# A transformer block's MLP computed with seven half products in place of eight

## The chip, the cores and the metric

The kernel runs on one core of a Trainium2 chip, as one launch. The metric is the device time of that launch in microseconds (us). TensorE (PE) multiplies and accumulates in PSUM, VectorE (DVE), ScalarE (ACT) and GpSimd (POOL) work element by element, SyncE (SP) issues most of the DMAs. PSUM tiles ps_A, ps_B, ps_C and ps_D are 128x1024 float32 each, that is two halves of 128x512.

## The reference, cut to what matters

Two transformer blocks run on x (1 x 1024 tokens x 1024 features, float32). The change lies in the last layer: its MLP and the final norm, with D_FF = 4096.

```python
mix = jnp.concatenate([na_out.astype(x.dtype), ret_out], axis=-1)
x = x + mix @ w_out[l]
h = rms_norm_2(x, norm_mlp[l])
x = x + jnp.square(jax.nn.relu(h @ w_up[l])) @ w_down[l]
return rms_norm_2(x, norm_final)
```

## The kernel before

Activations lie transposed: X is [128, 8, 1024], eight tiles of 128 features by 1024 tokens. A float32 product is made of three products in a faster format: each operand is split into a rounded part (hi) and the rest (lo), and hi*hi + hi*lo + lo*hi is accumulated. `linear` makes one output tile of 128 features by 1024 tokens: 8 k-steps, 3 hi/lo products, 2 halves of 512 tokens, so 48 matmuls, alternating between the two halves of ps_A or ps_B. They are all recorded at line 525. A weight tile (128x1024, 512 KB) is loaded by SP into w_raw (L382), rounded to w_hi on POOL (L442) and its rest w_lo made by POOL (L435). Two such sets alternate; PE frees one by `lin_done`, POOL gives it by `w_ready`, PSUM tiles go by `ab_free`.

The MLP runs in four chunks (FF_CHUNKS) of 1024 inner features. `up` makes 8 tiles of h @ w_up from HA (hi and lo of the normed X). DVE takes each out with relu and the norm's factor rstd into ta (L2195), ACT squares it (L1534) and rounds it into HB_hi (L1536), DVE makes HB_lo (L2198). `down` makes 8 tiles from HB, and DVE adds each to X (L2204). That is 64 tiles, 3072 matmuls. Chunks but one run in hardware loops. The normed input is made while the layer's mixer output product (8 tiles) runs: DVE adds a tile to X (L1724), ACT scales and rounds it and squares it (L1025, L1029), DVE makes the lo part (L1589) and adds up the squares (L1593). The sum over features is a matmul with a tile of ones (L545), after the first `up` tile. ACT makes rstd from it by Ln and Exp (L1013, L1015).

After the last tile comes the final norm: squares (ACT L1547), their sum (DVE L2219), ones matmuls (L545), rstd, then the scaling of eight tiles, five on DVE (L2226) and three on POOL (L496), and eight output DMAs (L420).

Each engine runs its own program in order; only the semaphores tie them. The order in which an engine's code is written is the order of its work.

## Time and profile before

| | |
|---|---|
| median of 3 runs | 2687.0 us (2684.63 to 2688.97) |
| the profiled execution, its own time | 2685.58 us |
| its span, first to last instruction | 2683.8 us |
| MLP on PE, first to last matmul | 1955.35 to 2653.44 us of the span |
| PE busy over the span | 94% |

The span is what the trace shows; the time holds 1.8 us more that lie around it. Stages are given in microseconds from the span's start. "Idle before, releaser" in a row is the time that the engine stood still before the instruction and who ended it.

### The profile page before, as it was taken

Reading aid. Unit: us, or ns where it says so; the run is one execution under the profiler, and the core shown is the slowest. Engines: PE = TensorE matmul, PEld = TensorE weight load, DVE = VectorE, ACT = ScalarE, POOL = GpSimd, SP = SyncE. Lnnn points to the kernel's source line nnn. Section 1 sums busy time; section 2 is a strip of 40 time slices with the busy share of each in tenths; the row PEclk is TensorE's granted clock in tenths of the full one; section 3 lists DMA queues with packets and bytes.
Section 4 is the critical chain, followed back from the end, with each engine's and each line's share of the span. In section 5 each row is a group of like instructions: output and inputs, shape, how many; then the busy total and the mean of one; then the engine's idle time right before and its main releaser. Section 6 shows DMA issues by size and latency. Waiting matters only on the chain.

```text
span 2683.8 us, 31485 instructions
## 1 busy us (share of the span) xinstructions
PE 2525.6 (94%) x11924; PEld 1953.8 (73%) x11924; DVE 1249.2 (47%) x1673; ACT 849.0 (32%) x1263; POOL 852.5 (32%) x437
## 2 busy tenths in 40 slices
PE   7999669999999999998899999999999999999995
PEld 5877448776776677765767777787788888888884
DVE  6999863435545455454744655454421121121223
ACT  5555441324444444445332233213221010010111
POOL 2888743222222222221222221221333333333332
PEclk9999879999999999999999999999999999999998
DMA  3111201111111111111111211220111111111111
GB/s 124 48 47 43 77 21 47 67 38 53 39 37 36 31 36 39 44 36 29 34 57 46 50 44 33 81 71 24 47 47 48 48 55 48 47 47 47 47 50 67
DMA packets 70876, 129.48 MB, mean 48 GB/s; under 512 B 37880, under 2 KB 40952, under 8 KB 70776
## 3 DMA queue, kind: packets, MB, share of 16 engines
q1 hardware_dynamic: 30096, 107.27, 12.3%
q10 hardware_dynamic: 40680, 20.76, 3.4%
q8 instruction: 76, 1.25, 0.2%
q14 instruction: 24, 0.20, 0.0%
HBM read 117.39 MB, written 4.33 MB: 45 GB/s over the span
## 4 chain that ended last, share of the span: by engine, by line
PE 74%; DVE 10%; issue 6%; ACT 5%; POOL 2%; ACTq 1%; DVEq 0%; DMA 0%; SPq 0%; POOLq 0%
PE ps_A L525 34%; PE ps_B L525 27%; PE ps_B L599 2%; POOL ta L460 2%; PE ps_C L622 1%; PE ps_D L622 1%; PE ps_C L545 1%; PE ps_D L545 1%; PE ps_B L732 1%; ACT sc L1221 1%; DVE ssum L1593 1%; DVE ps_C L1639 1%; PE ps_B L545 1%; DVE sc L1774 1%; PE ps_C L708 1%
## 5 line engine op out<-in xcount | busy, mean ns | idle before, releaser
L442 POOL CAST w_hi<-w_raw 128x1024 fp32r<-128x1024 f32 x162 | 171.3, 1058 | 1657.8 <-PE ps_A L525 794.5
L435 POOL TENSOR_TENSOR w_lo<-w_raw,w_hi 128x1024 fp32r<-128x1024 f32 x188 | 467.2, 2485 | 60.2 <-ACT w_hi L1036 47.2
L525 PE MATMUL ps_A<-HA_hi,w_hi 128*128 128x512 f32 x960 | 314.7, 409 | 46.7 <-POOL HA_lo L484 21.1
L525 PE MATMUL ps_A<-HA_lo,w_hi 128*128 128x512 f32 x960 | 300.6, 395 | 0.0
L525 PE MATMUL ps_A<-HA_hi,w_lo 128*128 128x512 f32 x960 | 299.9, 394 | 0.0
L525 PE MATMUL ps_B<-HA_hi,w_hi 128*128 128x512 f32 x832 | 265.5, 400 | 3.6 <-DVE G L1620 3.3
L525 PE MATMUL ps_B<-HA_lo,w_hi 128*128 128x512 f32 x832 | 256.9, 390 | 0.0
L525 PE MATMUL ps_B<-HA_hi,w_lo 128*128 128x512 f32 x832 | 256.6, 390 | 0.0
L525 PEld LDWEIGHTS ps_A<-HA_hi,w_hi 128*128 128x128 f32 x960 | 176.5, 191 | 96.1 <-issue 47.5
L525 PEld LDWEIGHTS ps_A<-HA_lo,w_hi 128*128 128x128 f32 x960 | 182.9, 191 | 39.4
L525 PEld LDWEIGHTS ps_A<-HA_hi,w_lo 128*128 128x128 f32 x960 | 182.8, 190 | 39.6
L525 PE MATMUL ps_A<-HB_hi,w_hi 128*128 128x512 f32 x640 | 203.4, 399 | 7.0 <-DVE HB_lo L2063 4.2
L1534 ACT ACTIVATE sq<-ta 128x1024 f32<-128x1024 f32 x32 | 34.0, 1062 | 529.7 <-DVE ta L2195 529.7
L525 PE MATMUL ps_A<-HB_lo,w_hi 128*128 128x512 f32 x640 | 198.1, 391 | 0.0
L525 PE MATMUL ps_A<-HB_hi,w_lo 128*128 128x512 f32 x640 | 197.7, 390 | 0.0
L525 PEld LDWEIGHTS ps_B<-HA_lo,w_hi 128*128 128x128 f32 x832 | 156.3, 188 | 33.3
L525 PEld LDWEIGHTS ps_B<-HA_hi,w_lo 128*128 128x128 f32 x832 | 156.2, 188 | 33.2
L525 PEld LDWEIGHTS ps_B<-HA_hi,w_hi 128*128 128x128 f32 x832 | 152.0, 188 | 37.7 <-issue 8.6
L525 PE MATMUL ps_B<-HB_hi,w_hi 128*128 128x512 f32 x512 | 160.8, 395 | 0.0
L525 PE MATMUL ps_B<-HB_lo,w_hi 128*128 128x512 f32 x512 | 157.8, 389 | 0.0
L525 PE MATMUL ps_B<-HB_hi,w_lo 128*128 128x512 f32 x512 | 157.7, 389 | 0.0
L525 PEld LDWEIGHTS ps_A<-HB_hi,w_hi 128*128 128x128 f32 x640 | 118.4, 188 | 35.3 <-issue 8.2
(335 smaller groups left out, 3800.6 us busy)
## 6 DMA issues: line engine op xcount, KB each, us to landing
w_raw<-w_dram SPq DMA_DIRECT2D x188, 512.0 KB, 3.5
X<-x_dram SPq DMA_DIRECT2D x8, 512.0 KB, 8.0
X<-x_dram ACTq DMA_DIRECT2D x8, 512.0 KB, 7.2
out_dram<-X SPq DMA_DIRECT2D x8, 512.0 KB, 2.8
wp_sb<-wp_dram ACTq DMA_DIRECT2D x16, 128.0 KB, 2.0
qT<-q_in ACTq DMA_DIRECT2D x48, 32.0 KB
kT<-k_in ACTq DMA_DIRECT2D x48, 32.0 KB
p_A<-p_dram ACTq DMA_DIRECT2D x2, 512.0 KB, 3.9
```

Source lines behind the costliest of these rows:

```text
L435: pool.tensor_tensor(w_lo[q][:, :, :], w_raw[q][:, :, :], w_hi[q][:, :, :].bitcast(F32), ALU.subtract).then_inc(S[f"w_ready{q}"], 1)
L442: pool.tensor_copy(w_hi[q][:, :, :], w_raw[q][:, :, :]).then_inc(S["w_rounded"], 1)
L460: pool.tensor_tensor(accp[u][:, :], (tap_out[0] if j == 0 else accp[u])[:, :], tap_out[(j + 1) % 2][:, :], ALU.add).then_inc(S["pool_tap"], 1)
L525: op = pe.matmul(AB[b][:, cols], wt[:, w0 + k, :], act[:, k, cols], start=(first and k == ks[0] and step == 0), stop=(last and k == ks[-1] ...
L545: op = pe.matmul(ps[b][:, cols], m[:, :], src[:, cols], start=first, stop=last)
L599: op = pe.matmul(AB[b][:, cols], wp_sb[t][:, k, :], p_sb[k][:, cols], start=(k == 0), stop=(k == PLE_K - 1))
L622: op = pe.transpose(CD[b][:, c * P:(c + 1) * P], src(c), ident[:, :])
L708: op = pe.matmul(CD[slots[u]][d, T - P:T], V[:, k0 + c, d], pt[u % 2][:, (h * nk + c) * P:(h * nk + c + 1) * P], start=(c == 0), stop=(c = ...
L732: op = pe.matmul(AB[other][:, at:at + nk * P], qT[rows, u * P:(u + 1) * P], kT[rows, k0 * P:(k0 + nk) * P], start=True, stop=True)
L1221: op = act.activation(s, s, ACT.Exp, scale=-1.0, bias=st_at(g, u, h, 0), accum_out=st_at(g, u, h, 1))
L1534: act.activation(sq[:, :], ta[:, :], ACT.Square).then_inc(S["u_sq"], 1)
L1593: dve.tensor_tensor(ssum[:, :], ssum[:, :], sq[:, :], ALU.add).then_inc(S["ssum_added"], 1)
```

## The change

The MLP's two products are each cut into 2x2 blocks: output features, inner index and tokens each in two halves. In place of the eight block products of each such group come seven (Strassen's algorithm in Winograd's form), on sums and differences of blocks. One block product (`half_product`) is 12 matmuls of 128x128 by 128x512: 4 k-steps of 3 hi/lo products, all into one half of a PSUM tile. Products x = 1 to 7 are run in an order in which later ones accumulate onto earlier ones in PSUM ("running sums").

Up: 16 pairs of output tiles (UP_PAIRS), seven products each. Left blocks are weights (DVE makes s1 to s4 from the raw weights), ACT rounds each (up_w hi, a ring of five) and POOL makes its lo part. Right blocks are sums of halves of the normed X, formed once (HT, seven operands with hi and lo) at the end of the mixer's output product. ACT copies running sums out (`keep_p1`, `keep_u2`, `keep_p5`), DVE adds and applies relu (c11, c22, c12, b21), ACT squares, and DVE forms differences (t1, b12, t2, t4). The seven combinations per pair are stored to u_dram by SP, 256 KB each.

Down: the combinations are read back (`t_piece`, 512 KB each), split into hi and lo again on ACT and DVE, four operands in flight. Items are (products, chunk, pair of output tiles): 48 items of two products in three phases (1,2), (6,5), (7,3) and 16 items of product 4 alone. Weights of each pair are loaded again in every phase: 512 KB, 768 KB, 1 MB and 256 KB an item, a ring of three. DVE forms their sums (`form_item`: none, two, three and none), ACT rounds, POOL makes lo.

X is stored to memory ahead of the up products and loaded again in the down stage, since the up stage uses its place. The final norm is made for each half of the tokens; the second half's is made before the last items are done. Some other semaphores are merged, and the constant tile perm is no longer loaded. The loops of this part are gone from every program (PE's has 5016 rows in place of 3121).

```diff
+UP_PAIRS = FF_CHUNKS * KH
+UP_ORDER = [(0, x) for x in (1, 5, 6, 2, 7)]
+for _i in range(1, UP_PAIRS):
+    UP_ORDER += [(_i, 1), (_i - 1, 3), (_i - 1, 4)]
+    UP_ORDER += [(_i, x) for x in ((5, 6, 2, 7) if _i < UP_PAIRS - 1 else (6, 5, 7, 2, 3, 4))]
+UP_AT = {_s: _n for _n, _s in enumerate(UP_ORDER)}
+RING = 5
...
+PHASES = ((1, 2), (6, 5), (7, 3))
+CHUNKS = len(PHASES) * FF_CHUNKS
+ITEMS = CHUNKS * PAIRS
...
+            def up_weights(i):
+                c, b = divmod(i, KH)
+                for t in range(2):
+                    sp.dma_start(a_raw[i % 2][t][:, :, :], w[MLP_AT + 2 * KT * c + b + KH * t]) \
+                        .then_inc(S[f"a_loaded{i % 2}"], 16)
+            def store_u(i, x, tile):
+                c, b = divmod(i, KH)
+                sp.dma_start(u_dram[x - 1, c, :, b, :], tile[i % 2][:, :]).then_inc(S[f"u_stored{i % 2}"], 16)
+            def store_two(i):
+                sp.wait_ge(S["b_ready"], 4 * i + 2)
+                store_u(i, 1, b11)
+                store_u(i, 3, b22)
+            def store_five(i):
+                sp.wait_ge(S["t_formed"], 4 * i + 4)
+                store_u(i, 2, b21)
+                store_u(i, 5, t1)
+                store_u(i, 7, b12)
+                store_u(i, 6, t2)
+                store_u(i, 4, t4)
...
+            def t_piece(k):
+                t, h = divmod(k, 2)
+                if k < 2:
+                    sp.wait_ge(S["up_split"], UP_AT[(UP_PAIRS - 2, 4)] + 1)
+                elif k < 4:
+                    sp.wait_ge(S["up_split"], len(UP_ORDER))
+                else:
+                    sp.wait_ge(S["t_ready"], k - 3)
+                c = t // 2 % FF_CHUNKS if t < 2 * CHUNKS else t - 2 * CHUNKS
+                for q in range(2):
+                    sp.wait_ge(S[f"u_stored{q}"], 16 * 7 * (KH // 2) * (c + 1))
+                sp.dma_start(t_raw[k % 4][:, :, :], u_dram[T_ORDER[t] - 1, c, :, 2 * h:2 * h + 2, :]) \
+                    .then_inc(S[f"t_loaded{t % 2}"], 16)
...
+                kind, c, p = item(i)
+                if i < 2:
+                    sp.wait_ge(S["up_done"], UP_AT[(UP_PAIRS - 1, 7)] + 1)
+                elif i == 2:
+                    sp.wait_ge(S["up_done"], UP_AT[(UP_PAIRS - 1, 3)] + 1)
+                else:
+                    sp.wait_ge(S["down_split"], split_count(i - 2))
...
+            for i in range(UP_PAIRS - 1):
+                if i > 0:
+                    sp.wait_ge(S["up_split"], UP_AT[(i - 1, 4)] + 1)
+                    up_weights(i + 1)
+                store_two(i)
+                if i > 0:
+                    store_five(i - 1)
+            store_five(UP_PAIRS - 2)
+            for k in range(4):
+                t_piece(k)
+            for i in range(3):
+                down_weights(i)
+            store_two(UP_PAIRS - 1)
+            store_five(UP_PAIRS - 1)
+            for i in range(LAST):
+                if i >= 3:
+                    down_weights(i)
+                for k in t_pieces_after(i):
+                    t_piece(k)
+                if i == PAIRS + 1:
+                    for q in range(2):
+                        sp.wait_ge(S[f"u_stored{q}"], 16 * 7 * UP_PAIRS // 2)
+                    for k in range(KT):
+                        sp.dma_start(X[:, k, :], out[k]).then_inc(S[f"x_loaded{k}"], 16)
...
+            for s in range(len(UP_ORDER)):
+                hi, lo = up_w[s % RING]
+                pool.wait_ge(S["up_hi"], s + 1)
+                pool.tensor_tensor(lo[:, :, :], up_source(s), hi[:, :, :].bitcast(F32),
+                                   ALU.subtract).then_inc(S["up_split"], 1)
+            for i in range(LAST):
+                for j, x in enumerate(item(i)[0]):
+                    hi, lo = down_w[i % 3][j]
+                    pool.wait_ge(S["down_hi"], split_count(i) + j + 1)
+                    pool.tensor_tensor(lo[:, :, :], d_raw[i % 3][:, down_parts(x), :], hi[:, :, :].bitcast(F32),
+                                       ALU.subtract).then_inc(S["down_split"], 1)
...
-            def down():
-                def u_ready(k):
-                    pe.wait_ge(S["u_ready"], n.next("u_ready"))
-                linear(0, HB, pre=u_ready)
-                for t in range(1, KT):
-                    linear(t % 2, HB)
-            opening(0, HA)
-            for t in range(1, KT):
-                linear(t % 2, HA)
-            down()
-            with n.loop(pe, FF_CHUNKS - 1, w_ready0=8, w_ready1=8, ab_free0=8, ab_free1=8, u_ready=KT):
-                for t in range(KT):
-                    linear(t % 2, HA)
-                down()
-            norm_stats()
...
+            def half_product(bank, wt, ht, first, ready=None):
+                for k in range(KH):
+                    if ready:
+                        ready(k)
+                    for step, (a, b) in enumerate(((wt[0], ht[0]), (wt[0], ht[1]), (wt[1], ht[0]))):
+                        op = pe.matmul(bank, a[:, k, :], b[:, k, :], start=(first and k == 0 and step == 0),
+                                       stop=(k == KH - 1 and step == 2), skip_group_check=True)
+                return op
...
+            for s, (i, x) in enumerate(UP_ORDER):
+                q = i % 2
+                if x == 1:
+                    bank = AB[q][:, HALVES[0]]
+                    if i < 2:
+                        pe.wait_ge(S[f"ab_free{q}"], n.now(f"ab_free{q}"))
+                    else:
+                        pe.wait_ge(S["up_out"], OUT_AT[("r21", i - 2)] + 1)
+                if x == 6:
+                    bank = AB[q][:, HALVES[0]]
+                    pe.wait_ge(S["kept"], KEPT_AT[(1, i)] + 1)
+                if x == 7:
+                    bank = AB[q][:, HALVES[0]]
+                    pe.wait_ge(S["kept"], KEPT_AT[(6, i)] + 1)
+                if x == 4:
+                    bank = AB[q][:, HALVES[0]]
+                    pe.wait_ge(S["up_out"], OUT_AT[("c22", i)] + 1)
+                if x == 5:
+                    bank = AB[q][:, HALVES[1]]
+                    if i >= 2:
+                        pe.wait_ge(S["up_out"], OUT_AT[("c12", i - 2)] + 1)
+                if x == 3:
+                    bank = AB[q][:, HALVES[1]]
+                    pe.wait_ge(S["kept"], KEPT_AT[(5, i)] + 1)
+                if x == 2:
+                    bank = CD[0][:, HALVES[q]]
+                    if i == 0:
+                        pe.wait_ge(S["cd_free0"], n.now("cd_free0"))
+                    elif i >= 2:
+                        pe.wait_ge(S["up_out"], OUT_AT[("c11", i - 2)] + 1)
+                pe.wait_ge(S["up_split"], s + 1)
+                ready = (lambda k: pe.wait_ge(S["mlp_lo"], LO_AT[(x, k // 2 if x in (7, 4) else k)] + 1)) if i == 0 else None
+                half_product(bank, up_w[s % RING], HT[x], x in (1, 2, 5), ready).then_inc(S["up_done"], 1)
+                if (i, x) == (0, 6):
+                    norm_stats()
...
+            def round_up(s):
+                i, x = UP_ORDER[s]
+                if s >= RING:
+                    act.wait_ge(S["up_done"], s - RING + 1)
+                if x in (1, 2, 4):
+                    act.wait_ge(S[f"a_loaded{i % 2}"], 32 * (i // 2 + 1))
+                else:
+                    act.wait_ge(S["up_sum"], SUM_AT[(i, x)] + 1)
+                act.copy(up_w[s % RING][0][:, :, :], up_source(s)).then_inc(S["up_hi"], 1)
...
+            for i in range(1, UP_PAIRS):
+                s = UP_AT[(i, 1)]
+                round_up(s + 3)
+                squared(b22, i - 1, "r22")
+                round_up(s + 4)
+                keep_p1(i)
+                round_up(s + 5)
+                squared(b12, i - 1, "r12")
+                round_up(s + 6)
+                squared(b21, i - 1, "r21")
+                if i < UP_PAIRS - 1:
+                    keep_p5(i)
+                    round_up(s + 7)
+                    keep_u2(i)
+                    round_up(s + 8)
+                    round_up(s + 9)
+                else:
+                    keep_u2(i)
+                    keep_p5(i)
+                    round_up(s + 7)
+                    round_up(s + 8)
+                squared(b11, i, "r11")
...
+            def form_s1(i):
+                dve.wait_ge(S[f"a_loaded{i % 2}"], 32 * (i // 2 + 1))
+                if i > 0:
+                    dve.wait_ge(S["up_split"], UP_AT[(i - 1, 5)] + 1)
+                second = a_raw[i % 2][1]
+                dve.tensor_tensor(s1[:, :, :], second[:, 0::2, :], second[:, 1::2, :], ALU.add).then_inc(S["up_sum"], 1)
+                dve.wait_ge(S["up_sum"], SUM_AT[(i, 5)] + 1)
+            def form_s2_s3(i):
+                first, second = a_raw[i % 2]
+                if i > 0:
+                    dve.wait_ge(S["up_split"], UP_AT[(i - 1, 6)] + 1)
+                dve.tensor_tensor(s2[:, :, :], s1[:, :, :], first[:, 0::2, :], ALU.subtract).then_inc(S["up_sum"], 1)
+                dve.tensor_tensor(second[:, 0::2, :], second[:, 0::2, :], first[:, 0::2, :],
+                                  ALU.subtract).then_inc(S["up_sum"], 1)
...
+            def c11(i):
+                stage_free(i)
+                dve.wait_ge(S["up_done"], UP_AT[(i, 2)] + 1)
+                dve.wait_ge(S["kept"], KEPT_AT[(1, i)] + 1)
+                dve.tensor_tensor(b11[i % 2][:, :], p1[:, :], CD[0][:, HALVES[i % 2]], ALU.add).then_inc(S["up_out"], 1)
+                out(("c11", i))
+                relu(b11, i, 0, b11[i % 2][:, :])
...
+            def form_t(i):
+                q = i % 2
+                dve.wait_ge(S["b_ready"], 4 * i + 4)
+                dve.tensor_tensor(t1[q][:, :], b12[q][:, :], b11[q][:, :], ALU.subtract).then_inc(S["t_formed"], 1)
+                dve.wait_ge(S["t_formed"], 4 * i + 1)
+                dve.tensor_tensor(t2[q][:, :], b22[q][:, :], t1[q][:, :], ALU.subtract).then_inc(S["t_formed"], 1)
+                dve.tensor_tensor(b12[q][:, :], b12[q][:, :], b22[q][:, :], ALU.subtract).then_inc(S["t_formed"], 1)
+                dve.wait_ge(S["t_formed"], 4 * i + 2)
+                dve.tensor_tensor(t4[q][:, :], b21[q][:, :], t2[q][:, :], ALU.subtract).then_inc(S["t_formed"], 1)
...
+            c11(0)
+            r22(0)
+            for i in range(1, UP_PAIRS):
+                if i > 1:
+                    c22(i - 1)
+                    r22(i - 1)
+                form_s4(i)
+                c12_c21(i - 1)
+                if i < UP_PAIRS - 1:
+                    form_s1(i + 1)
+                    form_s2_s3(i + 1)
+                form_t(i - 1)
+                c11(i)
...
+            def form_item(i):
+                kind, raw = item(i)[0], d_raw[i % 3]
+                if kind in PHASES[1:]:
+                    dve.wait_ge(S[f"d_loaded{i % 3}"], down_loads(i))
+                if kind == (6, 5):
+                    dve.tensor_tensor(raw[:, A21, :], raw[:, A21, :], raw[:, A22, :], ALU.add).then_inc(S["down_formed"], 1)
+                    dve.wait_ge(S["down_formed"], sums_formed(i) + 1)
+                    dve.tensor_tensor(raw[:, A11, :], raw[:, A21, :], raw[:, A11, :],
+                                      ALU.subtract).then_inc(S["down_formed"], 1)
+                if kind == (7, 3):
+                    dve.tensor_tensor(raw[:, A21, :], raw[:, A21, :], raw[:, A11, :],
+                                      ALU.subtract).then_inc(S["down_formed"], 1)
+                    dve.tensor_tensor(raw[:, A12, :], raw[:, A12, :], raw[:, A22, :],
+                                      ALU.subtract).then_inc(S["down_formed"], 1)
+                    dve.wait_ge(S["down_formed"], sums_formed(i) + 2)
+                    dve.tensor_tensor(raw[:, A12, :], raw[:, A12, :], raw[:, A21, :],
+                                      ALU.subtract).then_inc(S["down_formed"], 1)
```

PE at the seam between two output tiles, before (HB is the inner operand; an "x2" row is the two halves of ps_A or ps_B):

```order
L525 MATMUL ps_B<-HB_hi,w_hi_57 128x512 x2
L525 MATMUL ps_B<-HB_lo,w_hi_57 128x512 x2
L525 MATMUL ps_B<-HB_hi,w_lo_59 128x512 x2
L532 REGISTER_ALU
L507 REGISTER_ALU
L525 MATMUL ps_A<-HB_hi,w_hi_56 128x512 x2
L525 MATMUL ps_A<-HB_lo,w_hi_56 128x512 x2
```

and in the change, at the seam between products 6 and 2 of the first pair (ht is the right operand, up_w the weights):

```order
L1199 MATMUL ps_A<-ht_hi,up_w_hi 128x512
L1199 MATMUL ps_A<-ht_lo,up_w_hi 128x512
L1199 MATMUL ps_A<-ht_hi,up_w_lo 128x512
L785 MATMUL ps_D<-ssum,ones 128x512 x2
L1199 MATMUL ps_C<-ht_hi,up_w_hi 128x512
L1199 MATMUL ps_C<-ht_lo,up_w_hi 128x512
```

A matmul no longer comes twice with the same weights: twelve different ones go to one half of a tile.

SP's queue in the MLP, before (a loop over two weight tiles, then the outputs):

```order
L382 ISA [waits w_ready0]
L382 DMA w_raw_54<-w_dram 128x1024
L382 ISA [waits w_ready1]
L382 DMA w_raw_55<-w_dram 128x1024
L137 REGISTER_ALU
L137 COMPARE_AND_BRANCH
L420 DMA out_dram<-X 128x1024 [waits out_ready] x5
```

and in the change, one pair of the up stage (a_raw are raw weights, the rest the seven combinations of two pairs):

```order
L550 DMA a_raw10_173<-w_dram 128x1024 [waits up_split]
L550 DMA a_raw11_174<-w_dram 128x1024
L556 DMA u_dram<-b110_194 128x512 [waits b_ready]
L556 DMA u_dram<-b22s_208 128x512
L556 DMA u_dram<-b211_199 128x512 [waits t_formed]
L556 DMA u_dram<-t11_203 128x512
L556 DMA u_dram<-b121_197 128x512
L556 DMA u_dram<-t21_205 128x512
L556 DMA u_dram<-t41_207 128x512
L550 DMA a_raw00_171<-w_dram 128x1024 [waits up_split]
```

The next weights now stand behind seven stores and behind the wait on b_ready.

DVE in the change, one pair of the up stage (s are weight sums, b and t the combinations, u and p kept sums):

```order
L2739 TENSOR_TENSOR b22s<-b22s,ps_A 128x512 [waits kept,up_done]
L2718 SCALAR_TENSOR_TENSOR b22s<-b22s,rstd 128x512 [waits up_out]
L2713 TENSOR_TENSOR s_187<-a_raw_173,s_186 128x512 [waits up_sum,up_split]
L2750 TENSOR_TENSOR b_196<-u_189,ps_A 128x512 [waits kept,up_done]
L2718 SCALAR_TENSOR_TENSOR b_196<-b_196,rstd 128x512 [waits up_out]
L2754 SCALAR_TENSOR_TENSOR b_198<-ps_A,rstd 128x512 [waits up_done]
L2696 TENSOR_TENSOR s_185<-a_raw_172 128x512 [waits up_split,a_loaded0]
L2704 TENSOR_TENSOR s_186<-s_185,a_raw_171 128x512 [waits up_split,up_sum]
L2705 TENSOR_TENSOR a_raw_172<-a_raw_172,a_raw_171 128x4x128
L2761 TENSOR_TENSOR t_202<-b_196,b_194 128x512 [waits b_ready]
L2763 TENSOR_TENSOR t_204<-b22s,t_202 128x512 [waits t_formed]
L2764 TENSOR_TENSOR b_196<-b_196,b22s 128x512
```

DVE had two instructions a tile here before; it now waits for the next pair's weights (a_loaded) in the middle of the row.

## Rows read from the trace of the kernel before

**Rows 1.** The page's head: span; busy time, share and instructions of each engine.
```profile
span 2683.8 us, 31485 instructions
PE 2525.6 (94%) x11924; PEld 1953.8 (73%) x11924; DVE 1249.2 (47%) x1673; ACT 849.0 (32%) x1263; POOL 852.5 (32%) x437
```
**Rows 2.** Busy time by stage: the MLP, and its end; PEclk is the granted clock.
```profile
1955.00:2654.00 699.00, 698.42 (x3078) 577.29 (x3076) 129.30 (x106) 81.92 (x77) 221.49 (x126) 1.00 0.14 46
2600.00:2684.00 84.00, 56.92 (x240) 45.09 (x238) 26.84 (x18) 14.23 (x13) 25.66 (x11) 0.86 0.16 62
```
**Rows 3.** Chain in order of time: start, us, what; first and last of 64 tiles.
```profile
1955.35 10.88 PE ps_A L525 x48
...
2642.55 10.89 PE ps_B L525 x48
```
**Rows 4.** PE in order of time: ones matmuls in the stream, and at the end.
```profile
1966.07 1.88 PE L545 MATMUL ps_D<-ssum,ones 128*128 128x512 f32 x4
...
2657.20 3.49 PE L545 MATMUL ps_C<-ssum,ones 128*128 128x512 f32 x4 [3.78 <-DVE ssum L2219]
```
**Rows 5.** The same chain, after the last tile.
```profile
2654.60 1.23 DVE ssum L2219
...
2657.16 0.04 issue
...
2660.73 1.11 ACT rstd L1013
...
2661.86 1.28 ACT L1015
...
2664.24 3.46 DVE X L2226
2667.71 3.28 DVEq L167
2670.99 5.67 DVE X L2226 x3
```
**Rows 6.** DVE groups (count, total and mean ns), and one tile's durations (min/median/max).
```profile
L2204 DVE TENSOR_TENSOR X<-X,ps_A 128x1024 f32<-128x1024 f32 x16 | 19.5, 1221 | 136.1 <-PE ps_A L525 136.1
...
L1774 DVE CUSTOM_DVE_ANT_0 sc<-ps_B,mask x112: 285/419/427, 643.4 to 1170.2; 128x256 f32<-128x256 f32 x74, 128x128 f32<-128x128 f32 x38
```
**Rows 7.** DVE, then POOL, in order of time, 199 to 239 us: both at work.
```profile
199.76 1.23 DVE L1650 TENSOR_TENSOR Y<-Y,ta 128x1024 f32 x1
201.22 1.29 DVE L1639 SCALAR_TENSOR_TENSOR ps_D<-ypad,dw_sb,ps_D 128x1024 f32<-128x1024 f32 x1 [0.23 <-DVE Y L1650]
202.41 1.28 DVE L1639 SCALAR_TENSOR_TENSOR ps_C<-ypad,dw_sb,ps_C 128x1024 f32<-128x1024 f32 x1
...
234.00 3.43 DVE L1650 TENSOR_TENSOR Y<-Y,accp 128x1024 f32 x1 [0.24 <-DVE ypad L1620]
...
199.83 3.42 POOL L460 TENSOR_TENSOR accp<-accp,tap_out 128x1024 f32<-128x1024 f32 x1 [1.34 <-ACT tap_out L1069]
...
233.96 2.39 POOL L460 TENSOR_TENSOR ta<-ta,tap_out 128x1024 f32<-128x1024 f32 x1 [1.35 <-ACT tap_out L1069]
```
**Rows 8.** ACT groups: total, mean ns.
```profile
L1231 ACT COPY pt<-ps_D 128x512 f32<-128x512 f32 x32 | 18.4, 576 | 15.7 <-PE ps_D L622 15.1
L1536 ACT CAST HB_hi<-sq 128x1024 fp32r<-128x1024 f32 x32 | 33.6, 1051 | 1.0
```
**Rows 9.** POOL: durations of the weights' lo parts, ns min/median/max.
```profile
L435 POOL TENSOR_TENSOR w_lo<-w_raw,w_hi x188: 2341/2402/3423, 12.6 to 2632.9; 128x1024 fp32r<-128x1024 f32 x188
```
**Rows 10.** DMA: KB each and us to landing; a stretch (last column GB/s); SP's issues.
```profile
w_raw<-w_dram SPq DMA_DIRECT2D x188, 512.0 KB, 3.5
...
10.00:15.00 5.00, 0.00 (x0) 0.00 (x0) 4.24 (x4) 4.90 (x6) 2.39 (x1) 1.00 1.02 415
...
3.22 3.65 SPq L391 DMA_DIRECT2D X<-x_dram  x7
```
**Rows 11.** DMA busy tenths and GB/s, 40 slices of 2655 to 2684 us: stores.
```profile
DMA  0000000000000000003940079002999999999940
GB/s 0 0 0 0 0 0 0 0 0 0 0 0 0 0 0 0 0 0 124 401 198 0 0 311 407 6 0 119 401 413 390 424 395 390 401 418 401 418 170 0
```
**Rows 12.** PE: small matmuls in order of time, then groups with mean ns.
```profile
651.65 0.66 PE L708 MATMUL ps_D<-pt,V 128*64 128x128 f32 x8
...
L708 PE MATMUL ps_D<-pt,V 128*64 128x128 f32 x320 | 28.5, 291 | 6.3 <-ACT pt L1231 6.3
...
L525 PE MATMUL ps_A<-HA_hi,w_hi 128*128 128x512 f32 x256 | 78.8, 389 | 0.0
```

566 lines of the change are left out of this document (487 added, 79 removed).

## The prediction

> **What bounds the kernel now.** I read the page's head first: PE is busy for 94% of a span of 2683.8 us, no other engine for half of it [rows 1]. Since the change lies in the MLP alone, I then read the busy time by stage. From 1955 to 2654 us PE is busy for 698.4 of 699 us at full clock, while DVE has 129 us of work, ACT 82 and POOL 221, and the DMAs run at 46 GB/s [rows 2]. The chain in order of time shows what one output tile costs: 10.88 us for 48 matmuls, from 1955.35 to 2642.55 + 10.89 = 2653.44 [rows 3]. So one matmul costs 10.88/48 = 0.2267 us, and the stage is 64 x 10.88 = 696.3 plus 1.9 for the ones matmuls [rows 4]. In it only the number of matmuls counts, as long as the others keep up. Behind 2653.44 the chain leaves PE: 30.4 us of norm, scaling and output [rows 5].
>
> **What is removed.** Up and down now have 112 half products each, 224 x 12 = 2688 matmuls in place of 3072. 384 x 0.2267 = **87.0 us less**. One half product is u = 2.72 us, a pair of the up stage 7u = 19.04 us, an item of two products 5.44 us.
>
> **The tail.** Before it is, from the last matmul: DVE, ACT and DVE again to 2657.16, ones matmuls 3.5 at 0.86 mean clock, Ln 1.11, a table load 1.28, Exp 1.06, scaling 12.4 (3.46 + 3.28 + 5.67), and 7.1 to the end [rows 2, 4, 5]. After it is for one half of the tokens: read-out 0.69, square 0.58, half of 1.88 for the ones, Ln 0.56, table 1.28, Exp 0.53, hops 0.3, scaling 6.2 (half), end 6.5 (half a DMA's bytes less). That is 17.6: **12.8 us less**.
>
> **Prices of the new work.** A DVE instruction of 512 elements: 1.221 us at 1024 and 0.285 at 128 give 0.69 [rows 6]. Of two that depend on each other the second starts 0.24 us behind the first; two that don't overlap by 0.09 (1.28 us each, 1.19 apart) [rows 7]. ACT takes 0.58 for 512 and 1.05 for 1024 [rows 8], POOL 2.40/2 = 1.20 [rows 9]. A DMA lands in 3.5 us for 512 KB; at the 415 GB/s of the startup 1.3 of them are the bytes, 2.2 are fixed [rows 10]. Stores reach 390 to 424 GB/s too [rows 11].
>
> **DVE and POOL share something.** A DVE instruction with two SBUF operands took 3.43 us beside a POOL instruction that had begun 0.04 us before, and 1.23 where it came first; then POOL took 3.42 in place of 2.40. With an operand in PSUM DVE kept its 1.28 us all the time [rows 7]. POOL's own 2.40 then began at 199.83 + 1.02 = 200.85, 0.14 before DVE's end at 200.99; so one that waits is let in 0.14 us early. Most of the new DVE work has two SBUF operands. Sums of durations: up, a pair: 11 such DVE instructions and 7 of POOL, 11 x 0.69 + 7 x 1.20 = 16.0 of 19.04 us. Down, four items (21.8 us of PE): phase (7,3) 12 x 0.69 + 4 x 1.23 + 8 x 1.20 = 22.8; phase (6,5) 20.0; phase (1,2) 14.5. Less 24 x 0.14, (7,3) needs 19.4: it fits, so I take no loss from this sum itself, only from single waits.
>
> The Trainium skill (SBUF — State Buffer, Who interferes with whom) says that a DVE instruction with two SBUF inputs and a GpSimd one that reads SBUF exclude each other, and that the second is blocked for the whole of the first. The trace agrees but for the 0.14 us. By the rule's letter (7,3) would need its 22.8 us, 4 us more in its four chunks than by the rows.
>
> **Up stage, steady.** PE runs (i,1), (i-1,3), (i-1,4), (i,5), (i,6), (i,2), (i,7). Whether it waits depends on one loop. SP issues the weights of pair i+1 behind seven stores, and these wait for the square of b22 of pair i-1. Seven stores of 256 KB and two loads of 512 KB are 2.88 MB, 7.0 us at 415 GB/s, + 2.2 = 9.2. (SP's own issues, 3.65/7 = 0.52 us each [rows 10], go on beside it.) Then DVE, in order, does s1, s2, s3, t1, t2, b12, t4, c11, r11, c22, r22: 11 x 0.69 - 6 x 0.09 + 4 x 0.24 = 8.0; ACT squares, 0.7; 0.2 until SP goes on. Sum 18.1 of 19.04 us. Contention with POOL comes on top, at up to 1.2 us for each POOL instruction that falls into the chain. But PE needs c22(i) only at (i,4), 24.5 - 19.0 - 0.7 = 4.8 us later than the earliest, and when DVE's chain slips by that, ACT's rounding for the next products (and so POOL's) lies ahead of it: one POOL instruction is left. That makes 19.3 against 19.04: 14 pairs x 0.3 = **4 us**, bounds 0 and (three POOL instructions in the chain, 21.7) 37 - 5 = 32 us.
>
> **Start of the up stage.** Take t = 0 at the end of the last mixer tile. The first two products are ready. The third's operand waits for DVE 1.22, T2 0.69, ACT, two z's and its lo part on DVE: at 4.1, due 5.4. Then ACT is the queue: T2's hi until 2.7, four scaled tiles 5.2, p1 5.8, a square of 1024 6.9, the weights of product 2 7.5, z 8.6, u2 (after product 6, 8.2) 9.2. The ones matmuls follow product 6; only behind them ACT rounds for product 7 (10.4), scales four tiles for operand 3 (12.9) and rounds the second z (14.0), and DVE has its lo part at 15.2 where PE is due at 13.7. Ln and Exp with two table loads of 1.28 hold ACT from 15.9 to 20.6, so product (0,3) waits to 22.6. DVE has s1, T4, their lo parts, s2, s3, c11, r11 in a row until 30.8, ACT squares b11 and only then rounds for (1,5): at 33.3, in place of 8 x 2.72 + 1.9 = 23.7. That is 9.6 us late, and 1.4 for contention: **11 us**, bounds 6 and 16. Before, nothing waits there [rows 2].
>
> **Seam between up and down.** The operands of the second chunk are loaded by SP behind store_five(15), which waits for form_t(15), that is for the last up product at 24.5 (from the start of (15,1)) and then r21, a square, four differences: 30.5. Five stores and two pieces, 2.36 MB: 5.8 + 2.2, so 38.6. ACT rounds the pieces ahead of the weights of item 2, which are ready at 41.7 and due at 24.5 + 10.9 = 35.4. PE stands 6.3 us. Behind an idle time of 3.78 us the ones matmuls took 3.49, in the stream 1.88 [rows 4], so the clock was at its lower level, 1.2 GHz; here about 2 us more for that. **8 us**, bounds 3 and 15. X's reload (4.2 MB, 10 us of DMA) delays item 6 to 61 us, due at 64: nothing.
>
> **Down, steady.** An item's weights are issued when POOL is done with the item three before, 16.3 us ahead. Load 4.9 (1 MB), three DVE sums 2.2, ACT 1.2, POOL 2.4, hops: 11 to 12, up to 15 with a piece ahead in the queue and some contention. In (7,3) DVE's order puts sums behind the pieces' lo parts, and that item comes about 1 us late in each chunk. Products 4 (2.72 us each): ACT rounds two pieces and squares four halves in the first four, 2 us late. **6 us** in all, bounds 0 and 30.
>
> **The sum.** 87.0 + 12.8 - 4 - 11 - 8 - 6 = 70.8. The profiled execution had 2685.6 and lies 1.4 below the median of 2687.0: 2614.8 there, **2616 us** against the median.
>
> **Rivals.**
> - *Up stage bound by the weights' loop* (14%): DMA or contention make it 21.2 us instead of 19.3. For it: it has 0.9 us to spare. Against: it moves POOL out of its way. 2.2 x 14 - 5 = 26 in place of 4: 2638.
> - *Down stage bound by DVE and POOL together* (10%): the sum of 22.8 holds and hand-overs cost as much again, and a late item also delays the next load; 24 us in place of 21.8 in the eight chunks of (6,5) and (7,3), 18 in place of 4: 2630. For it: both waits in [rows 7]. Against: the 0.14.
> - *Matmuls into one half of PSUM wait for each other* (5%, this one ends slower): no row shows twelve of 512 columns in a row in one half, before they alternate. 2688 of them at 26 ns more (70.8/2688) eat the whole gain; if each waited for the end of the last, 0.389 in place of 0.227 us, the time would be near 3050. Against: small ones that accumulate in one place stand (0.66 - 0.29)/7 = 53 ns apart, while each lasts 0.29 us [rows 12]. Taken at nothing. Nearly all of what is left for slower is here.
> - *The waits at the seams hide* (5%): DVE free of contention, pieces earlier: 15 us less, 2601.
> - Several of these at once (4%): 2655 to 2682.
> - That fewer matmuls are not run can be excluded: the order of PE's rows has them.
>
> **How the numbers follow.** The forecast case holds 62%, with a range of its own of 2600 to 2632. The range 2598 to 2652 takes in most of the first two rivals; outside are the 5% slower, the 4% of mixtures, a part (4%) of the first rival and 3% below. 0.2% (5.4 us) is about what a measurement can tell from no change. Faster: all but the PSUM rival and half of the mixtures, 0.93; same 0.02; slower 0.05.
>
> **What would show it.** Rows of 12 matmuls at 2.72 us in the chain; if 3 or more, the PSUM rival. In the up stage a distance of (i,1) to (i+1,1) of 19.0 to 19.5; 21 and PE waiting for DVE's b22 or for POOL's lo part of product 5 means the first rival, with the wait of s1 for a_raw's DMA before it. PE idle 8 to 12 us in the first 35 us and 5 to 9 us in one piece at the third item. In phase (7,3) DVE's sums at 1.5 us and more instead of 0.69 and items of more than 6 us mean the second. A tail of 17 to 19 us behind the last matmul. I am wrong if PE's matmuls slow down, or if stalls add up to more than 60 us; then a queue that I took for hidden sets the pace.

## The result and the profile after

The changed kernel takes **2719.14 us** (median of 4 runs, 2716.19 to 2723.24); the kernel before took 2687.33 beside it. The ratio is 1.012, with a 95% interval of 1.0101 to 1.0139: 1.2% slower. I had forecast 2616 us, in a range of 2598 to 2652, and gave slower a chance of 0.05. The profiled execution had 2723.24 us, 37.7 more than that of before.

The page's head for the changed kernel:

```profile
span 2721.4 us, 31649 instructions
...
PE 2479.9 (91%) x11542; PEld 1901.0 (70%) x11542; DVE 1558.3 (57%) x2025; ACT 1035.3 (38%) x1623; POOL 971.7 (36%) x533
```

PE has 384 matmuls less and still ends later, so it stands. The busy time by stage says where (columns: stretch, length, busy us of PE, PEld, DVE, ACT and POOL, then PE's granted clock, the DMA share, GB/s):

```profile
2000.00:2100.00 100.00, 89.51 (x367) 71.53 (x365) 53.50 (x60) 31.66 (x57) 46.54 (x30) 0.94 0.51 125
2100.00:2200.00 100.00, 84.09 (x336) 67.38 (x336) 53.66 (x62) 31.90 (x58) 45.31 (x29) 0.93 0.50 117
2200.00:2300.00 100.00, 86.73 (x339) 69.36 (x340) 52.99 (x62) 32.20 (x59) 46.20 (x29) 0.90 0.48 116
2300.00:2360.00 60.00, 45.98 (x192) 36.73 (x191) 33.16 (x38) 18.31 (x33) 23.91 (x16) 0.91 0.61 156
2360.00:2400.00 40.00, 25.56 (x98) 20.28 (x98) 16.55 (x14) 13.42 (x21) 17.91 (x12) 0.80 0.65 193
2400.00:2500.00 100.00, 98.86 (x436) 81.28 (x435) 46.07 (x41) 38.64 (x54) 51.18 (x35) 1.00 0.70 253
```

The number of matmuls is the one to read: 336 to 367 in 100 us of the up stage, 436 in the down stage. At 0.2267 us each, 441 would fit. The MLP on PE now runs from 1961.4 to 2705.05, 743.7 us where it was 698.1 [rows 3]; 2688 matmuls are 609.4 of it, so PE stands or runs at a lower clock for 134 us (1.9 of them are the ones matmuls, as before). By place, each time taken from the starts of matmuls less 2.72 us for each half product: the start of the up stage (1961.39 to 1997.26, 8 half products) 12; **the up stage's steady part (to 2351.73, 103 half products) 74**; the seam (to 2389.68, 5 half products) 24, of which two stops, below, are 22; the down stage (to 2705.05, 108 half products) 22, of which 12 are stops.

In the steady part a pair takes 24.2 to 25.8 us (median 24.5) in place of 19.04. Of its 74 us, 46 are 13 stops of PE, one in each pair, each before product 7. Most of the rest are matmuls at the lower clock behind these stops: from 2127.40 to 2130.40 us, for example, the granted clock is 0.50 (1.2 GHz), and matmuls start 0.43 us apart there and 0.23 afterwards.

```profile
2126.54 0.50 PE L1199 MATMUL ps_A<-ht_hi,up_w_hi 128*128 128x512 f32 x1 [3.26 <-ACT u L1857]
...
2127.46 0.63 PE L1199 MATMUL ps_A<-ht_hi,up_w_hi 128*128 128x512 f32 x1
2127.88 0.63 PE L1199 MATMUL ps_A<-ht_lo,up_w_hi 128*128 128x512 f32 x1
...
2130.98 0.39 PE L1199 MATMUL ps_B<-ht_hi,up_w_hi 128*128 128x512 f32 x1
```

What sets the length of a pair is seen on the other engines. SyncE's rows show one turn (start, duration, queue, line, out<-in, count):

```profile
2136.37 0.33 SPq L556 DMA_DIRECT2D u_dram<-b  x1
...
2138.72 1.34 SPq L556 DMA_DIRECT2D u_dram<-t  x2
2140.11 1.32 SPq L550 DMA_DIRECT2D a_raw<-w_dram  x2
2160.65 1.30 SPq L556 DMA_DIRECT2D u_dram<-b  x3
```

From the first store to the next turn's first store it is 24.3 us. DVE's rows between them:

```profile
2149.60 0.69 DVE L2696 TENSOR_TENSOR s<-a_raw 128x512 f32<-128x512 f32 x1 [9.49 <-DMA a_raw<-w_dram]
2150.33 0.69 DVE L2704 TENSOR_TENSOR s<-s,a_raw 128x512 f32<-128x512 f32 x1
2150.94 1.77 DVE L2705 TENSOR_TENSOR a_raw<-a_raw,a_raw 128x512 f32<-128x512 f32 x1
2152.64 1.77 DVE L2761 TENSOR_TENSOR t<-b,b 128x512 f32<-128x512 f32 x1
2154.43 1.67 DVE L2763 TENSOR_TENSOR t<-b22s,t 128x512 f32<-128x512 f32 x1
2156.03 0.68 DVE L2764 TENSOR_TENSOR b<-b,b22s 128x512 f32<-128x512 f32 x1
...
2159.26 0.69 DVE L2718 SCALAR_TENSOR_TENSOR b<-b,rstd 128x512 f32<-128x512 f32 x1
```

and GpSimd's:

```profile
2150.35 1.81 POOL L724 TENSOR_TENSOR up_w_lo<-a_raw,up_w_hi 128x512 fp32r<-128x512 f32 x1 [8.65 <-ACT up_w_hi L1849]
2152.12 1.73 POOL L724 TENSOR_TENSOR up_w_lo<-s,up_w_hi 128x512 fp32r<-128x512 f32 x1
2153.82 1.74 POOL L724 TENSOR_TENSOR up_w_lo<-a_raw,up_w_hi 128x512 fp32r<-128x512 f32 x1
```

So the loop is the one that I had named: stores and loads 13.2 us (2136.37 to 2149.60), DVE from s1 to r22 10.35 (to 2159.95), ACT's square and the hop back 0.7. Over 13 turns the first term is 13.1 to 14.7 us (13.6 in the mean), and the other two together are 11.0 to 11.1 in every one. What surprised me were the sizes, 13.2 for my 9.2 and 10.35 for my 8.0. Where PE feels it, the view of waits says for 2010 to 2270 us (who waits <- for whom: us in total, times, longest):

```profile
DVE s L2696 <- DMA a_raw<-w_dram: 96.8, 10, 10.7
ACT b L1865 <- DMA u_dram<-t: 29.2, 4, 7.7
PE ps_B L1199 <- ACT u L1857: 19.4, 5, 4.4
ACT up_w_hi L1849 <- DMA a_raw<-w_dram: 16.7, 10, 2.6
PE ps_A L1199 <- ACT u L1857: 14.5, 5, 3.4
```

PE waits for ACT's copy u2 (L1857), and in ACT's program that copy stands behind `round_up(s + 7)`, which waits for the load of the next weights. Ahead of both stands the copy of p5 (L1865), which waits until the stores of the pair two before have landed, in the turn shown until 2147.74. The seam has two stops:

```profile
2359.70 0.79 PE L1199 MATMUL ps_B<-ht_hi,up_w_hi 128*128 128x512 f32 x1 [7.97 <-DVE b L2739]
...
2389.68 0.77 PE L1199 MATMUL ps_B<-ht_hi,down_w_hi 128*128 128x512 f32 x1 [14.44 <-issue]
```

The tail came as forecast. The chain's last twelve matmuls end at 2705.05, 16.3 us before the end; before it was 30.4 [rows 5].

```profile
2702.27 2.78 PE ps_B L1199 x12
```

### The profile page after: what moved, and what is told of

The parts are those of the page before. It is cut to its first block and busy times, and to the rows that moved or that the text cites. A ratio compares the mean times of both kernels' runs of the same rounds, so it can differ in the third digit from the quotient of the medians.

```text
span 2721.4 us, 31649 instructions
## 1 busy us (share of the span) xinstructions
PE 2479.9 (91%) x11542; PEld 1901.0 (70%) x11542; DVE 1558.3 (57%) x2025; ACT 1035.3 (38%) x1623; POOL 971.7 (36%) x533
## 5 line engine op out<-in xcount | busy, mean ns | idle before, releaser
L662 POOL TENSOR_TENSOR w_lo<-w_raw,w_hi 128x1024 fp32r<-128x1024 f32 x124 | 311.4, 2511 | 56.2 <-ACT w_hi L1339 48.4
L765 PE MATMUL ps_A<-HA_hi,w_hi 128*128 128x512 f32 x704 | 234.5, 415 | 49.0 <-POOL HA_lo L711 23.0
L730 POOL TENSOR_TENSOR down_w_lo<-d_raw,down_w_hi 128x512 fp32r<-128x512 f32 x112 | 164.3, 1492 | 185.8 <-ACT down_w_hi L1969 185.7
L765 PE MATMUL ps_A<-HA_lo,w_hi 128*128 128x512 f32 x704 | 221.3, 396 | 0.0
L765 PE MATMUL ps_A<-HA_hi,w_lo 128*128 128x512 f32 x704 | 220.6, 395 | 0.0
L765 PE MATMUL ps_B<-HA_hi,w_hi 128*128 128x512 f32 x576 | 185.9, 404 | 3.6 <-DVE G L2086 3.3
L765 PE MATMUL ps_B<-HA_hi,w_lo 128*128 128x512 f32 x576 | 177.8, 390 | 0.0
L2855 DVE TENSOR_TENSOR ht_lo<-t_raw,ht_hi 128x1024 fp32r<-128x1024 f32 x56 | 85.3, 1562 | 120.3 <-ACT ht_hi L1953 120.3
L724 POOL TENSOR_TENSOR up_w_lo<-a_raw,up_w_hi 128x512 fp32r<-128x512 f32 x64 | 103.8, 1628 | 139.6 <-ACT up_w_hi L1849 139.0
L1371 ACT ACTIVATE tap_out<-ypad,act_dw 128x1024 f32<-128x1024 f32 x80 | 89.8, 1147 | 79.3 <-POOL ta L687 41.5
```

The costliest lines, as they stand in the source:

```text
L662: pool.tensor_tensor(w_lo[q][:, :, :], w_raw[q][:, :, :], w_hi[q][:, :, :].bitcast(F32), ALU.subtract).then_inc(S[f"w_ready{q}"], 1)
L724: pool.tensor_tensor(lo[:, :, :], up_source(s), hi[:, :, :].bitcast(F32), ALU.subtract).then_inc(S["up_split"], 1)
L730: pool.tensor_tensor(lo[:, :, :], d_raw[i % 3][:, down_parts(x), :], hi[:, :, :].bitcast(F32), ALU.subtract).then_inc(S["down_split"], 1)
L765: op = pe.matmul(AB[b][:, cols], wt[:, w0 + k, :], act[:, k, cols], start=(first and k == ks[0] and step == 0), stop=(last and k == ks[-1] ...
L1371: act.activation(tap_out[j % 2][:, :], ypad[u][:, at:at + T], ACT.Identity, scale=act_dw[:, at:at + 1]).then_inc(S["tap_product"], 1)
L2855: dve.tensor_tensor(dT[t % 4][1][:, ks, :], t_raw[k % 4][:, :, :], dT[t % 4][0][:, ks, :].bitcast(F32), ALU.subtract).then_inc(S["t_ready" ...
```

## The experiments

Sixteen kernels, each a small edit of the changed one. "before" was 2686 to 2689 us in each group of runs. One more, e4, was to halve the bytes of each store at the same number of packets; it gave no time, so whether bytes or packets make the stores slow is not measured.

| run | edit | us |
|---|---|---|
| changed kernel | | 2719.1 |
| e1 | loads ahead of stores | 2648.1 |
| e2 | ACT copies u2 earlier | 2718.5 |
| e3 | loads behind the stores' landing | 2732.4 |
| e5, e11, e13 to e17 | rows of the stores otherwise in memory | 2661.6, 2661.9, and below |
| e12 | e5, GpSimd's work cut | 2644.0 |
| e6 to e10 | e1 and more | 2646.0, 2645.9, 2641.7, 2632.0, 2626.0 |

### e1: take the loads out of the loop

```diff
             for i in range(UP_PAIRS - 1):
-                if i > 0:
-                    sp.wait_ge(S["up_split"], UP_AT[(i - 1, 4)] + 1)
-                    up_weights(i + 1)
+                if i < UP_PAIRS - 2:
+                    sp.wait_ge(S["up_split"], UP_AT[(i, 4)] + 1)
+                    up_weights(i + 2)
                 store_two(i)
```

> SyncE issues the raw weights of pair i+2 as soon as GpSimd is done with product (i,4), ahead of the stores of pairs i and i-1; nothing else is changed. Theory L (in the up stage the time of a pair, 24.5 us, is that of one loop: seven stores and two loads issued together, 13.2 us until the weights land, DVE's chain from s1 to r22 10.4 us, ACT's square 0.7): the loads leave the loop, the time of a pair falls to PE's own 19.04 us or a little above (19 to 20.5), 13 pairs x 4 to 5.4 us = 52 to 70 us less, so 2649 to 2667 us. Theory C (DVE and GpSimd, sharing access to SBUF, are what a pair's 24.5 us consist of): nothing but the place of the waits changes, 24 us a pair, 2710 to 2720. Theory K (ACT's order: u2 is copied out behind the rounding of the next pair's weights): as L, since the rounding has no load to wait for any more; e2 tells K from L.

Measured: 2648.14 us (2647.66 to 2655.98), 0.9859 of before (0.9832 to 0.9887). SyncE's rows of e1 stand 19.2 us apart:

```profile
2138.46 0.81 SPq L550 DMA_DIRECT2D a_raw<-w_dram  x2
2142.77 0.33 SPq L556 DMA_DIRECT2D u_dram<-b  x1
...
2157.73 0.81 SPq L550 DMA_DIRECT2D a_raw<-w_dram  x2
```

and the stretches are full at full clock:

```profile
2100.00:2200.00 100.00, 100.00 (x439) 82.20 (x438) 60.60 (x79) 40.35 (x73) 47.17 (x37) 1.00 0.56 155
```

The same stores, the same DVE and GpSimd work, and PE doesn't wait. So it was theory L: not the amount of any engine's work, but the closed loop that the order of SyncE's queue made. C is out. 71 us came back, 1 more than L's range allowed; counted as above, the steady part costs 4.2 us in e1 in place of 74.3.

### e2: is it ACT's order?

```diff
                     keep_p5(i)
+                    keep_u2(i)
                     round_up(s + 7)
-                    keep_u2(i)
                     round_up(s + 8)
```

> ACT copies the running sum u2 out ahead of rounding the weights of (i+1,1), which waits for their load; SyncE's order stays. Theory K: PE gets product (i,7) without waiting for the load, the stalls of 4 to 8 us behind u2 go, and the time of a pair falls to 20 to 21 us: 45 to 60 us less, 2660 to 2675. Theory L: the stall only moves to another place (c22 on DVE is behind s1, s2 and s3 of the next weights anyway), the time of a pair stays at 24 to 24.5 us and the kernel within 5 us of 2719.

Measured: 2718.45 us (2714.37 to 2724.26); turns of 24.3 us (first stores at 2133.06, 2157.29 and 2181.67). The range of theory L held. The edit takes the rounding out of the way of u2's copy, but not the copy of p5 before it, which still waits for stores to land (until 2144.23 in one turn, where the weights' load ends at 2146.3). So PE's stops before product 7 shrank from 45.7 to 30.9 us in 13 pairs, and new ones for c22 and for GpSimd's lo parts came to 16: the sum is 47 us, and the turn stayed. K is out, since PE waits as long in all with the rounding moved. Moving one of PE's waits doesn't shorten a loop that PE's work isn't part of.

### e3: why 13.2 us and not 9.2?

```diff
                 if i > 0:
                     sp.wait_ge(S["up_split"], UP_AT[(i - 1, 4)] + 1)
+                    sp.wait_ge(S[f"u_stored{(i - 1) % 2}"], 16 * (7 * ((i - 1) // 2) + 2))
+                    if i > 1:
+                        sp.wait_ge(S[f"u_stored{i % 2}"], 16 * 7 * (i // 2))
                     up_weights(i + 1)
```

> SyncE waits until the seven stores have landed before it issues the two loads. It separates two readings of the 13.2 us that seven stores (1.8 MB) and two loads (1 MB) took where I had 9.2. Theory M (loads from memory and stores to it at the same time slow each other): alone, the stores take 4.5 + 2.2 = 6.7 us and the loads 4.8, together 11.5, so a pair takes 22.5 to 24 us and the kernel 2700 to 2715. Theory R (stores whose rows are 2 KB in a partition are slow by themselves, about 8 us or more for the seven): 8 to 10 + 4.8 = 13 to 15 us, a pair 24.5 to 26.5, the kernel 2719 to 2745, and the trace shows 8 us or more from the first store's issue to the last one's landing with no load beside them.

Measured: 2732.43 us (2732.02 to 2737.01). From the first store to the loads' issue it was 9.2 us (2139.60 to 2148.82), and the loads had landed for DVE at 2153.71, 4.9 later: 14.1 in place of 13.2. The DMA row of e3 for 2139 to 2160, in 40 slices of 0.525 us:

```profile
DMA  0029999999999978300067899920000000000000
GB/s 0 0 98 382 367 254 324 375 234 261 246 187 234 172 144 183 66 0 0 0 148 234 335 359 414 375 109 23 0 0 0 0 0 0 0 0 0 0 0 0
```

The stores begin at 380 GB/s and fall, unevenly, to 144 to 260 with no load beside them, while the DMA engines stay about as busy (9 tenths at 382 GB/s and at 172, 7 at 144); the loads reach 414. So M's account is out (it wanted 6.7 us for the stores alone, and they took 9.2), and R, whose range held, is right as far as that the stores are slow by themselves. That loads beside them slow them further isn't excluded: a store of t lands in 5.6 us in e3 and e1 and in 7.6 in the changed kernel, with two loads queued right behind. There the same transfers (2136 to 2150 us, slices of 0.35) fall to 82 to 129 GB/s in the middle:

```profile
DMA  0005999999999999999999979899998788875000
GB/s 0 0 0 217 374 381 345 252 287 357 398 240 246 263 234 263 88 94 117 123 123 82 111 129 275 176 240 199 217 281 316 316 328 316 351 316 222 12 0 0
```

But in the changed kernel's tail (2708 to 2721 us), stores with rows of 2 KB, 4 KB apart, run at 360 to 400 GB/s, so it isn't the length of a row:

```profile
GB/s 0 0 0 0 0 0 0 0 0 0 0 0 0 0 0 113 365 328 0 0 44 397 353 13 0 13 359 372 397 384 378 378 366 403 372 384 372 391 271 0
```

### e5, e11, e13 to e17: where the rows lie

`u_dram` was (7, FF_CHUNKS, P, KH, HALF): the 128 rows of a store, 2 KB each, lie 8192 bytes apart. In e5 they follow each other:

```diff
-        u_dram = nc.dram_tensor("u_dram", (7, FF_CHUNKS, P, KH, HALF), F32, kind="Internal").ap()
+        u_dram = nc.dram_tensor("u_dram", (7, FF_CHUNKS, KH, P, HALF), F32, kind="Internal").ap()
-                sp.dma_start(u_dram[x - 1, c, :, b, :], tile[i % 2][:, :])
+                sp.dma_start(u_dram[x - 1, c, b, :, :], tile[i % 2][:, :])
```

> The changed kernel with its own order, but the combinations lie in memory so that a store's 128 rows of 2 KB follow each other; before, they stood 8 KB apart, and a t_piece is now read in rows of 2 KB instead of 4. In e3 the seven stores took 9.2 us with no load beside them, at 380 GB/s in the first 2.5 us and 150 to 250 behind them; the stores of the tail, rows of 2 KB too but 4 KB apart, ran at 360 to 400. Theory S (the distance of the rows slows the stores): 9.2 falls to 4.5 + 2.2 = 6.7, 2.5 us less in each of 13 loops, 32 us: 2687; that it arrives in full would also confirm that the loop binds. Rival Q (a queue filled with many transfers of 256 KB slows down wherever they go, or the reads of SBUF meet those of the engines): no change, 2714 to 2724; reading pieces in shorter rows may cost the down stage up to 5 us.

> The changed kernel with its own order; only the distance between a store's 128 rows in memory is 8704 bytes in place of 8192, the rows stay 2 KB and apart, and the pieces are read in rows of 4 KB as before. With rows that follow each other (e5) a pair took 20.7 us and the kernel 2661.6. Theory Z (a distance of 8192 bytes brings many rows onto the same part of the memory): as e5, 2656 to 2668. Rival G (any gap between the rows, or more pages touched, costs it): as the changed kernel, 2712 to 2722.

> The changed kernel with its own order, the rows of a store 16384 bytes apart in place of 8192. If a distance of a larger power of two uses fewer parts of the memory, the stores slow down by up to half again: seven take 12 to 17 us in place of 9.2, 4 to 8 us more a pair, 2770 to 2830. If 8192 bytes is already the worst case: 2712 to 2726.

> The changed kernel with its own order, rows of a store 4096 bytes apart. If only a distance of exactly 8192 bytes is slow, a store of t lands in 3.0 us (as at 2048, 8704 and 16384) and the kernel takes 2658 to 2672 us. If slowness has to do with rows that lie apart by a small power of two (4096 and 8192, no longer 16384): 5 to 8 us, 2690 to 2720. The stores of the tail, 4096 bytes apart, ran at 360 to 400 GB/s, so the first is likelier.

> Rows 12288 bytes apart (8192 + 4096). If 8192 alone is slow: t lands in 3.0 us, 2658 to 2672. If odd multiples of 4096 above it too: 2700 to 2720.

> Rows 32768 bytes apart. 16384 cost a little (loads landing in 5.3 us in place of 5.0, the kernel 8 us longer than with dense rows). If that is the beginning of a trend with the size of the region: 2675 to 2690, t at 3.5 us or more. If not: 2660 to 2672.

> Rows 8192 bytes apart as in the changed kernel, but the regions of the seven combinations lie 4 MB + 32 KB apart in place of 4 MB, so that stores in flight together no longer start at addresses equal in their low 22 bits. If stores that are in flight together collide with each other at this distance: t lands in 3 to 4 us, 2658 to 2680. If it is the distance within each store: 7.6 us as in the changed kernel, 2712 to 2724.

| run | rows apart, bytes | a store of t lands in, us | kernel, us (lowest, highest) |
|---|---|---|---|
| changed kernel | 8192 | 7.6 | 2719.1 (2716.2, 2723.2) |
| e17 | 8192, regions shifted by 32 KB | 6.6 | 2704.6 (2700.6, 2705.4) |
| e5 | 2048 | 3.0 | 2661.6 (2658.4, 2665.3) |
| e14 | 4096 | 3.1 | 2665.6 (2664.4, 2671.8) |
| e11 | 8704 | 3.0 | 2661.9 (2660.5, 2667.9) |
| e15 | 12288 | 3.0 | 2663.9 (2658.9, 2671.1) |
| e13 | 16384 | 3.0 | 2669.7 (2665.6, 2674.6) |
| e16 (two runs) | 32768 | 3.0 | 2663.7 (2662.6, 2664.8) |

The landing times are the page's, here of the changed kernel, with the loads (KB each, median us from issue to landing):

```profile
a_raw<-w_dram SPq DMA_DIRECT2D x32, 512.0 KB, 8.1
u_dram<-b SPq DMA_DIRECT2D x56, 256.0 KB, 3.4
u_dram<-t SPq DMA_DIRECT2D x48, 256.0 KB, 7.6
```

and of e5:

```profile
a_raw<-w_dram SPq DMA_DIRECT2D x32, 512.0 KB, 5.0
u_dram<-b SPq DMA_DIRECT2D x56, 256.0 KB, 2.5
u_dram<-t SPq DMA_DIRECT2D x48, 256.0 KB, 3.0
```

One loop's transfers in e5, 2118 to 2132 us in slices of 0.35, stay near 380 until the queue runs empty of stores:

```profile
GB/s 0 0 0 146 374 381 421 392 404 375 398 375 386 363 380 363 339 205 351 351 328 293 246 281 304 398 234 164 23 12 0 0 0 0 0 0 0 0 0 0
```

This turn's transfers take 10.4 us (2118.43 to 2128.81 on DVE). Over 13 turns it is 9.4 to 10.7 in e5 (9.8 in the mean) and 9.4 to 10.8 in e11 (9.9), in place of 13.6, and a pair takes 20.5 to 21.8 us. A change of the address alone, with no instruction moved, gave 57.5 us: 13 x 3.8 = 49 in the turns, and 8 in the two stops of the seam (8.0 and 14.4 became 5.0 and 9.4).

How the expectations fared: S was right on e5 in kind and gave half of the gain (2.5 us a turn, 2687). Z held on e11, and G is out. Both ranges for e13 missed: 16384 is neither worse than 8192 nor as bad. The first cases of e14 and e15 held, and the second of e16. e17 came between its two: 1.0 us less in a turn, 14.5 us in all. So of seven distances only 8192 bytes is slow, and about 15 of the 57 us hang on how the seven regions stand to each other. That the rest hangs on the distance within a store is the reading that is left, not shown: only one shift was tried, itself a multiple of 8192. What in the memory makes 8192 special these runs don't tell.

### e12: the other 2.35 us of the loop

```diff
             for s in range(len(UP_ORDER)):
                 hi, lo = up_w[s % RING]
                 pool.wait_ge(S["up_hi"], s + 1)
-                pool.tensor_tensor(lo[:, :, :], up_source(s), hi[:, :, :].bitcast(F32),
+                ks = slice(0, KH if s < 2 * RING else 1)
+                pool.tensor_tensor(lo[:, ks, :], up_source(s)[:, ks, :], hi[:, ks, :].bitcast(F32),
                                    ALU.subtract).then_inc(S["up_split"], 1)
```

> e5 (rows that follow each other, the changed kernel's own order; a pair takes 20.7 to 21.1 us), and from the eleventh product on GpSimd makes the lo part of only one of four k-steps (128 elements in place of 512; the other lo parts are stale, which is left out of the computation). In e5 DVE's chain from s1 to r22 takes 10.4 us, with three instructions at 1.67 to 1.79 in place of 0.69. Theory C2 (they wait for GpSimd's access to SBUF, and the chain lies in the loop): 3 x 1.0 less, 2 or so after what is left of the collisions, until PE's own 19.04 binds: 1.3 to 2 us in each of 12 pairs and 2 us at the start, 2636 to 2646. Rival H (the chain's length is DVE's own, or hidden): 2656 to 2662.

Measured: 2643.99 us (2641.86 to 2647.58), 17.6 less than e5. DVE's rows of e12, which answer to those of the changed kernel above:

```profile
2116.39 0.69 DVE L2697 TENSOR_TENSOR s<-a_raw 128x512 f32<-128x512 f32 x1 [3.33 <-DMA a_raw<-w_dram]
...
2117.73 0.95 DVE L2706 TENSOR_TENSOR a_raw<-a_raw,a_raw 128x512 f32<-128x512 f32 x1
2118.61 0.68 DVE L2762 TENSOR_TENSOR t<-b,b 128x512 f32<-128x512 f32 x1
2119.32 0.84 DVE L2764 TENSOR_TENSOR t<-b22s,t 128x512 f32<-128x512 f32 x1
...
2124.01 0.69 DVE L2719 SCALAR_TENSOR_TENSOR b<-b,rstd 128x512 f32<-128x512 f32 x1
```

The chain is 8.3 us (2116.39 to 2124.70), my 8.0 and a little; in it DVE now even waits 0.33 for PE, and a turn is 19.2 us (first stores at 2106.23, 2125.39, 2144.67). C2 holds: contention with GpSimd was 2 us of the loop (10.35 less 8.3). In the changed kernel it is no accident that three of GpSimd's instructions fall into DVE's chain: the landing of the weights releases DVE's s1 and, by way of ACT, GpSimd's lo parts together.

### e6 to e10: the seam, the start, and all of it

e6 is e1 with ACT rounding item 2 before the next chunk's pieces:

```diff
-                if i > 0:
+                if i > 0 and i != 2:
                     round_item(i)
+                if i == 1:
+                    round_item(2)
                 for k in t_pieces_after(i):
```

> e1 (loads first, 2648), and ACT rounds the weights of item 2 ahead of the first two pieces of the next chunk, for which it waited 16.3 us there while those weights had been in SBUF for 20 us. Theory O (ACT's order makes PE's 14.3 us of standing at item 2): they go, and what is next, item 4, needs the pieces 10.9 us later, so 10 to 14 us less and 1 or 2 of clock: 2633 to 2638. Rival D (the pieces come so late that item 4 stands in its place): under 5 us, 2643 to 2648.

Measured: 2646.02 us (2640.85 to 2653.33), 2.1 less than e1, with the ranges overlapping. The stop of 14.3 us at item 2 became one of 12.9 at item 3: its weights stand in ACT's program behind the same pieces. O named a true wait and the wrong cure; D's range held, with item 3 in place of item 4.

e7 adds to e6, in the order of the programs (the split of pieces 0 and 1 moves up on ACT and DVE with it):

```diff
+            t_piece(0)
+            t_piece(1)
             store_five(UP_PAIRS - 2)
-            for k in range(4):
-                t_piece(k)
-            for i in range(3):
-                down_weights(i)
+            down_weights(0)
+            t_piece(2)
+            t_piece(3)
+            down_weights(1)
+            down_weights(2)
```

> e6, and the first two pieces of the down stage are loaded ahead of the last five stores of pair 14, rounded and split ahead of DVE's wait for product (15,2), item 0's weights are loaded ahead of pieces 2 and 3, and c22(15) comes ahead of nothing but itself. In e1 PE stands 6.9 us before (15,4), for c22 behind two pieces on DVE. If that order is the cause, 6 us less than e6 and no new stall above 1 us at item 0: 2627 to 2632. Rival: item 0's weights and pieces, which lay hidden under those 6.9 us (landed at 2280 to 2284 with (15,3) done at 2277), now make PE stand at item 0: 1 to 4 us less, 2631 to 2637.

Measured: 2645.89 us (2643.75 to 2650.91): nothing, and neither range came. The 6.9 us before (15,4) are gone, and PE stands 2.7 at item 0, 2.7 at item 1 and 11.2 at item 3. The stop at item 0 is the rival's; the one at item 1 neither theory had. ACT's rows of e7 show the wait behind the last:

```profile
2309.47 1.99 ACT L1884 CAST ht_hi<-t_raw 128x1024 fp32r<-128x1024 f32 x2 [16.62 <-DMA t_raw<-u_dram]
...
2313.93 3.21 ACT L1974 CAST down_w_hi<-d_raw 128x512 fp32r<-128x512 f32 x6
```

e8 adds the start:

```diff
             keep_p5(0)
-            inverse_root(rstd[:, :], b, 1.0 / D, "rstd_ready")
             round_up(6)
             round_up(7)
+            inverse_root(rstd[:, :], b, 1.0 / D, "rstd_ready")
...
+            round_up(8)
             squared(b11, 0, "r11")
```

> e7, and at the start of the up stage ACT rounds the weights of (0,3) and (0,4) ahead of Ln and Exp with their table loads, those of (1,5) ahead of squaring b11(0), and DVE forms both halves of the fourth right operand before their lo parts. The stalls of 3.1, 2.0 and 3.4 us at (0,3), (0,4) and (1,5) are then to shrink. If ACT's queue is what sets them, 5 to 8 us less than e7: 2620 to 2626. Rival: rstd comes 1.2 us later and with it c11, r11 and all of DVE's row up to s2 and s3, so that the stalls move to (1,6) and (2,1): 0 to 3 us less.

Measured: 2641.66 us (2640.64 to 2648.14), 4 less, the ranges overlapping. The stops of 3.1, 2.0 and 3.4 us became 4.5 and 0.8: 3.2 us less, just over the rival's 0 to 3, where the first theory wanted 5 to 8.

e9 moves what the pieces stood behind in SyncE's queue:

```diff
             down_weights(2)
+            t_piece(4)
+            t_piece(5)
             store_two(UP_PAIRS - 1)
+            t_piece(6)
+            t_piece(7)
+            down_weights(3)
             store_five(UP_PAIRS - 1)
```

> e8, and SyncE issues the pieces of the second chunk and the weights of item 3 ahead of the stores of pair 15, which they don't need (those wait for the last product, r21 and four differences; the pieces hold pairs 4 to 7), and ACT rounds item 1 ahead of squaring b12 and b21 of pair 15. In e7 PE stood 11.2 us at item 3, for ACT had the pieces ahead of it and they landed at 2309 to 2312, and 2.7 us at item 1. Theory Q (what is left of the seam is the place in SyncE's queue): 11 to 13 us less than e8, 2628 to 2632. Rival: the loads now share the DMA engines and PE waits 3 to 6 us at items 2 to 4 instead: 2633 to 2638.

Measured: 2632.00 us (2628.34 to 2639.28), 9.7 less than e8, where theory Q wanted 11 to 13. The stop of 11.0 us at item 3 is gone, but the rival's kind is there too: in e9 PE stands 2.8 us at 2286, 2.4 at 2312 and 4.1 at 2328. e10 is e9 with e5's layout:

> e9 with the combinations in rows that follow each other in memory, as in e5. If the loads of weights were the only thing for which the stores' speed counted, they are out of the loop already and it gives 0 to 2 us. If slower stores also held item 0's weights (9 us from issue to landing in e7, beside five stores and two pieces) and the pieces: 3 to 6 us more, 2623 to 2629.

Measured: **2625.95 us** (2620.48 to 2626.99, 5 runs), 6.1 less than e9: the second case, the slow stores had also held loads at the seam. It is 0.9756 of before (0.9742 to 0.9770). That is 2.4% faster than the kernel before and 3.4% faster than the change as it was made. Two stretches of e10, up stage and seam; its largest stops left are 4.5 us at 1987 and 3.8 at 2315:

```profile
2100.00:2200.00 100.00, 100.00 (x440) 82.21 (x439) 62.17 (x78) 41.02 (x75) 48.82 (x37) 1.00 0.43 156
...
2260.00:2300.00 40.00, 40.00 (x178) 33.00 (x177) 25.88 (x25) 20.61 (x31) 20.22 (x14) 1.00 0.88 315
```

## Why the prediction was wrong, by its steps

- **384 matmuls less, 87.0 us: right.** In the down stage of the changed kernel the starts of matmuls in one half of PSUM stand 0.2267 us apart (436 in 98.9 busy us), so the rival in which they wait for each other is out.
- **Tail, 12.8 less: right**; 16.3 in place of 30.4 us is 14.1 less.
- **Start of the up stage, 11: right**, 12. A part of it is the wait for the fourth operand's lo part on DVE (2.0 us here, 4.5 in e8), which e8 moved but didn't remove.
- **Up stage, steady, 4 with bounds 0 and 32: wrong, 74.** This step decides the sign: had it cost 4, the profiled execution would have taken some 2653 us, 38 above the 2614.8 forecast for it and 32 below that of before. e1, where this part costs 4.2, takes 2648. The loop was the right one, three things in it were not.
  - *"2.88 MB, 7.0 us at 415 GB/s, + 2.2 = 9.2"*: it took 13.6 in the mean of 13 turns, 13.2 in the one shown. I had priced bytes by rates of loads, and of stores with other addresses, and had no bound for the case that the address matters. 3.8 us of the difference go with the rows' distance of 8192 bytes; with it mended 9.8 remain (e5; e11: 9.9).
  - *"one POOL instruction is left"*: three were, 10.35 in place of 8.0 (e12 gives 8.3 when they are short). I had let DVE slip away from them, but they are released by the same event as DVE's chain. My bound of 21.7 us had three of them in the chain, and still the 9.2 for the bytes. In the turn shown, 13.2 + 10.35 + 0.7 = 24.3, the two terms stand for 4.0 and 2.35.
  - *"PE needs c22(i) only at (i,4), 4.8 us later"*: taken off once, as in the bound (37 - 5), it may stand (no run isolates it), but the forecast of 19.3 used it in every pair to move GpSimd's work out of DVE's chain. In a closed loop (stores, loads, DVE, ACT, stores) DVE's slip moves the next stores and loads along, and with their landing GpSimd's work too: in each of 13 turns it was 11.0 to 11.1 us from s1 to the next store. If the loop's sum is above PE's time for a pair, PE waits by the difference in every pair.
- **Seam, 8 with bounds 3 and 15: too small, 24**, 22 of it stops. The stop at item 2 was rightly placed (ACT rounds pieces before its weights) but 14.4 in place of 6.3; e5's layout alone brought it to 9.4. In e1, where only the seam is left, r21 and the four differences came 8.3 us behind the last product's end (2288.6 to 2296.9) in place of 6.0, two of the differences taking 1.67 and 1.77 us each, and five stores and two pieces took 12.6 (to 2309.45) in place of 8.0. The other stop, 8.0 us, I had overlooked: c22(15) stands on DVE behind the lo parts of the first two pieces.
- **Down stage, 6 with bounds 0 and 30: 22**, inside the bounds. 12 are stops, the largest 3.5 us at 2578, 2.8 at 2667 and 1.6 at 2569; more than half of the rest are matmuls at the lower clock behind the larger ones and behind the seam's, a term that I had only for the seam. At the stops of 3.5 and 1.6 us DVE's rows have the sums (L2869 to L2874) behind lo parts of pieces that took 3.3 us for two in place of 2.4, which fits the cause given; no run isolates it.
- The rest is a later start of the MLP, 6.0 us (1961.4 for 1955.4), 5.7 of which were there at a matmul early in the mixer output product (1887.0 for 1881.4), ahead of the change's place; in e1, with the same program up to there, it is 1957.1. The sum -87 - 14 + 12 + 74 + 24 + 22 + 6 is 37, for 37.7 measured.

The rival of the weights' loop was the one that came, with the sign that I had named for it (s1 waiting for a_raw's DMA), and I gave it 14% and 2638, since I let it miss by 2.2 us a pair where it missed by 5.3 to 5.6. With the loads out of the loop (e1), or with both terms of the loop mended (e12), the forecast's picture appears: 19.2 us a pair, where I had said 19.3, and e10, with a better seam than I had assumed, ends at 2626 where the forecast was 2616.

The Trainium skill (SBUF — State Buffer, Who interferes with whom), on DVE and GpSimd excluding each other, agrees with e12 in kind. In the changed kernel's chain three instructions of 0.69 us took 1.67 to 1.77; with GpSimd's cut to a quarter they took 0.68 to 0.95.

## What to carry to other kernels

Look for closed loops across engines and queues, add up one turn, and compare it with the time of the engine that bounds; a late due time elsewhere helps once and not in each turn, and a misprice of the loop is paid in each turn. Put loads that depend only on a free buffer ahead of stores that wait for results: here that alone was 71 us. Where stores go to scratch memory, lay the rows of one store side by side, or look at the landing times of the first few; and when a wait is removed at a seam, find what else stands behind the same transfer before expecting the time.

## What the runs showed of the hardware

- Stores of 256 KB in 128 rows of 2 KB: with the rows 8192 bytes apart the rate of a queue of seven fell from 380 GB/s to between 144 and 260 (e3); at 2048, 4096, 8704, 12288, 16384 and 32768 bytes a store of t landed in 3.0 to 3.1 us in place of 7.6. Shifting the seven regions by 32 KB against each other gave back 1.0 us of it (e17).
- The DMA engines' busy share doesn't show this: it was 9 tenths at 382 GB/s and at 172 in e3, and 9 tenths at 82 to 123 GB/s in the changed kernel (2136 to 2150 us).
- Stops of 2.2 to 6.0 us in each pair also cost clock: 0.90 to 0.94 granted from 2000 to 2300 us in the changed kernel, where e1, without the stops, has 1.00 from 2000 to 2200. Behind the stop of 3.26 us before 2126.54 it was 0.50 from 2127.40 to 2130.40.
- A DVE instruction of 128x512 with two SBUF operands took 0.69 us alone and 1.67 to 1.77 beside GpSimd's of 128x512, which themselves took 1.73 to 1.81 (changed kernel, 2150 to 2156 us).
